# Turning the state-space input weights on TensorE: three rounded products of high and low parts in place of one in full precision

## The reference

```python
# 64 groups of 16 channels drive one 64-dim complex-diagonal state each
abar = exp(lam * dt);  f = (abar - 1) / lam
bb = f * B                        # (64 groups, 64 states, 16 channels), complex
s  = scan over time of  s[l] = abar * s[l-1] + bb @ u[l]
y  = Re(C @ s) + D * u            # then GELU and a sigmoid GLU
```

## Time and profile before

| what | value |
|---|---|
| median of three runs | 956.39 us |
| the profiled execution, its own time | 956.51 us |
| span of the profiled execution | 954.7 us |
| PE busy (matmul) | 933.3 us, 98% |
| DVE busy | 633.6 us, 66% |
| ACT busy | 349.0 us, 37% |
| mean granted TensorE clock | 0.999 |
| float32 matmuls of `part_a`, as records | 128 (96 into psa, 32 into psb) |

### The profile page before, as it was taken

How to read it: one execution, slowest core, us unless ns; L and a number is a source line. 1 busy time by engine, 2 the same in 40 slices (tenths; PEclk the granted TensorE clock), 3 DMA queues, 4 the chain that set the end, 5 groups by cost and what they waited for, 6 DMA issues and landing times.

```text
span 954.7 us, 11591 instructions
## 1 busy us (share of the span) xinstructions
PE 933.3 (98%) x4420; PEld 784.8 (82%) x4420; DVE 633.6 (66%) x904; ACT 349.0 (37%) x448; POOL 45.3 (5%) x82
## 2 busy tenths in 40 slices
PE   3999999999999999999999999999999999999997
PEld 3888888888888888888888888888888888888885
DVE  5988899877888884577677887665344444455233
ACT  5851353334444443345353535341022231223111
POOL 0019800000000000000000000000000000000000
PEclk9999999999999999999999999999999999999999
DMA  9843355446555354479474761696543258322222
GB/s 348 300 147 121 126 203 168 155 159 195 173 192 202 141 184 157 114 217 260 132 216 137 208 171 44 192 346 239 185 163 111 89 224 214 135 89 89 89 89 88
DMA packets 95143, 162.51 MB, mean 170 GB/s; under 512 B 38512, under 2 KB 55024, under 8 KB 95088
## 3 DMA queue, kind: packets, MB, share of 16 engines
q1 hardware_dynamic: 85728, 157.31, 50.4%
q10 hardware_dynamic: 9360, 4.46, 1.8%
HBM read 115.59 MB, written 46.14 MB: 169 GB/s over the span
## 4 chain that ended last, share of the span: by engine, by line
PE 97%; DVE 1%; DMA 1%; ACT 0%; SPq 0%; issue 0%; DVEq 0%
PE ps L1932 51%; PE ps L2052 18%; PE ps L2160 9%; PE psb L2052 8%; PE ps L2116 2%; PE psb L2105 1%; PE psb L2103 1%; PE psa L2091 1%; PE psa L2010 1%; PE psa L1932 1%; PE psb L1960 1%; DMA x_tok<-in_x 1%; PE ps L1960 0%; PE psb L2010 0%; PE psa L1960 0%; DVE par_w_p L534 0%
## 5 line engine op out<-in xcount | busy, mean ns | idle before, releaser
L1932 PE MATMUL ps<-bop,w_hi 128*128 128x512 f32 x1184 | 317.7, 390 | 0.2 <-DVE bop L1440 0.2
L1932 PEld LDWEIGHTS ps<-bop,w_hi 128*128 128x128 f32 x1184 | 221.3, 188 | 45.6 <-issue 0.3
L1932 PE MATMUL ps<-bop,w_lo 128*128 128x512 f32 x592 | 182.3, 389 | 0.0
L1932 PEld LDWEIGHTS ps<-bop,w_lo 128*128 128x128 f32 x592 | 111.1, 188 | 23.2
L1392 DVE TENSOR_TENSOR w_lo<-raw,w_hi 128x1024 fp32r<-128x1024 f32 x45 | 55.6, 1236 | 48.5 <-ACT w_hi L1010 48.4
L2052 PE MATMUL ps<-bop,r_hi 128*128 128x512 f32 x256 | 78.8, 389 | 0.0
L1010 ACT ACTIVATE w_hi<-raw 128x1024 fp32r<-128x1024 f32 x45 | 47.4, 1054 | 75.7 <-PE ps L1932 61.9
L2052 PEld LDWEIGHTS ps<-bop,r_hi 128*128 128x128 f32 x256 | 48.0, 188 | 10.0
L2052 PE MATMUL ps<-bop,r_lo 128*128 128x512 f32 x128 | 49.8, 389 | 0.0
L2160 PE MATMUL ps<-wo_hi,y_hi 128*128 128x512 f32 x128 | 49.8, 389 | 0.0
L2160 PE MATMUL ps<-wo_lo,y_hi 128*128 128x512 f32 x128 | 49.8, 389 | 0.0
(11 more groups left out here) (325 smaller groups left out, 1582.3 us busy)
## 6 DMA issues: line engine op xcount, KB each, us to landing
raw<-in_wstream SPq DMA_DIRECT2D x54, 512.0 KB, 4.5
pair_raw<-in_wstream SPq DMA_DIRECT2D x24, 512.0 KB, 4.2
ada<-in_w_ada SPq DMA_DIRECT2D x16, 512.0 KB, 11.5
x_tok<-in_x SPq DMA_DIRECT2D x8, 512.0 KB, 6.3
gs_d<-gt SPq DMA_DIRECT2D x8, 512.0 KB, 4.3
win_d<-win_new SPq DMA_DIRECT2D x8, 512.0 KB, 2.7
wout_d<-wout_new SPq DMA_DIRECT2D x8, 512.0 KB, 3.8
wout<-wout_d SPq DMA_DIRECT2D x8, 512.0 KB, 6.0
```

Source lines behind the costliest of these rows:

```text
L1932: last = mm(ps[slot(u)][:, f * HALF:f * HALF + HALF], a[:, k, :], b(k, f), start=k == order[0] and q == 0, stop=k == order[-1] and q == 2)
```

## The change

`v` and the C columns get a high and a low part. ACT rounds `v` to `v_hi` at the end of the iteration in which DVE made it; DVE subtracts to get `v_lo`, in the place of `v`, in the next iteration between `pair_low` P3 and the chunk at "a"; DVE makes `c_lo`, 128 x 128, right behind `v`. The identity and the high part of C are now of type fp32r. PE does three matmuls for each group: `v_hi` with [identity, C_hi] (144 columns), `v_lo` with the same (144 columns), `v_hi` with `C_lo` (16 columns, into the tap columns alone). `v_hi` lies where `vt` was, so `out_weights` takes a new scratch `wt`, at the place of `win_new`; for that reason it waits for the store of `win_new` before it, and `prep_out` on ACT now waits for `wout_ready`. The calls of `prep_out` and `part_a` at place "a", where no "in" chunk ever falls, are gone.

```diff
+        v_hi = at("v_hi", [P, GB, CH, SG], bop_at + 5 * TILE, F32R)
+        v_lo = at("v_lo", [P, GB, CH, SG], bop_at + 4 * TILE, F32R)
         win_new = at("win_new", [P, GB, P], p1[0])
+        wt = at("wt", [P, GB, CH, SG], p1[0])
...
+        c_lo = ssm("c_lo", [P, GB, SG], F32R)
...
-        eye_c = at("eye_c", [P, GB, P + SG], cur[0])
+        eye_c = at("eye_c", [P, GB, P + SG], cur[0], F32R)
...
+            def v_high(chunk):
+
+                if chunk is None or chunk[0] != "in":
+                    return
+                act.wait_ge(v_ready, chunk[1] + 1)
+                fn(v_hi[:, :, :, :], v[:, :, :, :], ACT.Copy).then_inc(v_hi_done, 1)
...
                 act.wait_ge(a_done, b + 1)
+                act.wait_ge(wout_ready, b + 1)
...
-                prep_out(CHUNK_AT.get((j, "a")))
...
                 if more:
                     pair_high(j + 1, P6)
+                v_high(CHUNK_AT.get((j, "b")))
...
-                    dve.wait_ge(wout_ready, KT)
+                    dve.wait_ge(a_done, KT)
...
                 tt(v[:, :, :, :], v[:, :, :, :], vt4, ALU.add).then_inc(v_ready, 1)
+                stt(c_lo[:, :, :], bc[:, 2, :, :], sign, eye_c[:, :, P:P + SG].bitcast(F32), ALU.mult, ALU.subtract).then_inc(v_lo_done, 1)
+
+            def in_weights_low(chunk):
+
+                if chunk is None or chunk[0] != "in":
+                    return
+                dve.wait_ge(v_hi_done, chunk[1] + 1)
+                tt(v_lo[:, :, :, :], v[:, :, :, :], v_hi[:, :, :, :].bitcast(F32), ALU.subtract).then_inc(v_lo_done, 1)
...
                 dve.wait_ge(wout_stored, 16 * b)
+                dve.wait_ge(cos_stored, 16)
+                dve.wait_ge(win_stored, 16 * b)
...
-                did(tt(vt4, bcast(cf[:, :, 24:32], 3, SG), bcast(bc[:, 3, :, :], 2, CH), ALU.mult))
+                did(tt(wt[:, :, :, :], bcast(cf[:, :, 24:32], 3, SG), bcast(bc[:, 3, :, :], 2, CH), ALU.mult))
                 do(tt(w, bcast(cf[:, :, 16:24], 3, SG), bcast(bc[:, 2, :, :], 2, CH), ALU.mult))
-                tt(w, w, vt4, ALU.add).then_inc(wout_ready, 1)
+                tt(w, w, wt[:, :, :, :], ALU.add).then_inc(wout_ready, 1)
...
                     pair_low(j, P3)
+                in_weights_low(CHUNK_AT.get((j - 1, "b")))
                 prepare(CHUNK_AT.get((j, "a")))
...
-                pe.wait_ge(v_ready, b + 1)
+                pe.wait_ge(v_lo_done, 2 * b + 2)
...
-                    vg = v[:, g, :, :].rearrange("p j h -> p (j h)")
+                    vh, vl = (z[:, g, :, :].rearrange("p j h -> p (j h)") for z in (v_hi, v_lo))
                     bank, at_ = turned[g]
-                    last = mm(bank[:, at_:at_ + P + SG], vg, eye_c[:, g, :], start=True, stop=True)
+                    mm(bank[:, at_:at_ + P + SG], vh, eye_c[:, g, :], start=True, stop=False)
+                    mm(bank[:, at_:at_ + P + SG], vl, eye_c[:, g, :], start=False, stop=False)
+                    last = mm(bank[:, at_ + P:at_ + P + SG], vh, c_lo[:, g, :], start=False, stop=True)
...
-                part_a(CHUNK_AT.get((j, "a")))
```

More of the change, by code:

```diff
@@ L404, in build @@
         pair_stored = two("pair_stored")
+        v_hi_done, v_lo_done = sem("v_hi_done"), sem("v_lo_done")
         v_ready, eye_ready, a_done, win_ready, win_stored = (sem("v_ready"), sem("eye_ready"), sem("a_done"),
```

## The result

The changed kernel took 962.52 us (median of four runs, 962.21 to 962.83) against 956.50 us for the kernel before, measured beside it: a ratio of 1.0063, 95% interval 1.0045 to 1.0080. It is slower by 6.0 us. The profiled execution took 962.52 us with a span of 960.5 us.

A forecast was written before the change was run, and what follows sets the result against it. PE's instruction pace was taken as the bound: 64 groups going from 245.0 to 333.9 ns add 5.7 us, ACT, DVE and queues nothing, giving 962.1 us. The range was 953.0 to 966.0, the likeliest case's own 961.3 to 965.7.

The forecast's parts named there:

- PE is the bound, and a change counts by PE's pace: Whole kernel: PE is 97% of the chain; a change counts by PE pace or by making PE wait.
- Each product at 111.3 ns: Bursts on PE: three products at the load-bound float32 pace, 333.9 ns a group against 245.0, +5.7 us over 64.
- The bound of 130 ns from one turn of type: Turn from float32 to fp32r on PE: load and handing over take 130 ns at most, 390 ns a group, +9.3 us.
- The rival of the hidden load: Three products of a burst: load takes 73 ns or less, kernel gains 5.0 to 1.6 us; chance 0.17.
- the even one: Products of a burst: a pace of 77 to 87 ns each keeps the difference within 1.1 us; chance 0.07.
- The rival without a single pass: Short fp32r products on PE: four passes like float32, +29.9 us (986) or +22.8 us (979); chance 0.05.
- The 0.06 us behind each burst as a price of changing type, taken as 0: Two half products behind each burst: 5.50 us against 5.44; if a type-change price, 0.5 us would go; taken as 0.
- ACT and DVE at nothing: v_hi 1.05 us on ACT, v_lo 1.24 and c_lo 0.28 on DVE: costed at nothing, working ahead of PE.
- the queue of SP at nothing: Stores of win_new and wout_new, loads of cf and bc: move by 0.7 to 1.2 us, costed at nothing.
- the faster rival: Three products of a burst: the load hides behind a short fp32r stream, 951.4 to 954.8 us; chance 0.17.
- The rival of the late `v_lo`: Top of each burst: PE waits for v_lo; 0.5 us at each of eight adds 4 us, 966; chance 0.06.

The follow-up runs named there:

- third_144: Changed kernel with the third product of each group moving 144 columns (identity and C_hi) in place of 16; 962.2 us, ratio 1.0061 to the kernel before.
- third_32cols: Changed kernel with the third product's stationary side 32 columns of v_hi in place of 128; 958.7 us, ratio 1.0028 to the kernel before.
- no_third: Changed kernel with the third product of each group (v_hi with C_lo, 16 columns) left out; 956.03 us, ratio 0.9997 to the kernel before.
- side_only: Changed kernel with its ACT and DVE work and waits, but one float32 product per group on PE; 956.82 us against 956.31 for the kernel before.
- v_lo_thrice: Changed kernel with two more operations of v_lo's size on DVE ahead of v_lo; 988.03 us, ratio 1.0324 to the kernel before.

## Why the prediction was right, step by step

The prediction said 962.1, the measured time is 962.52; against its own executions +5.7 was forecast and +6.0 measured, +5.8 by the spans.

- **PE is the bound, and a change counts by PE's pace.** Held: the 5.67 us of the loop are eight times the 0.71 of a burst.
- **Each product at 111.3 ns, the 16-column one too, 333.9 ns a group.** Held: 335 ns. That the load sets it was argued from two facts, that a load shrank as much as a two-pass stream between the slow and the fast stretch, and that an fp32r load is as long as a float32 one. third_144, third_32cols and no_third show it.
- **The bound of 130 ns from one turn of type.** Safe but loose: the pace measured is 111.8, and the 122.5 ns stream of the float32 record ahead would account for most of the 130.
- **The rival of the hidden load, and the even one.** Both fall. The stream alone would allow some 68 ns for 144 columns, which third_32cols laid bare, and the load's 112 stands above it. The fast weight load of the Trainium skill ("TensorE: Matmul & The Clock Gate", weight-path perf modes) did not show itself for fp32r: its load of 128 columns takes two cycles a column by the rows at half clock, and its record is as long as that of float32. The some 81 ns that the same page of the Trainium skill gives for a load and matmul pair of 128 columns (back-to-back issue gap) is not the pace here either: 111.8 ns.
- **The rival without a single pass.** Falls: 64 records more, not 256.
- **The 0.06 us behind each burst as a price of changing type, taken as 0.** Taking it as 0 was right. third_144 has no float32 product in the loop and its half products behind the burst still take 5.50 us, and in the changed kernel burst and half products exceed 24 x 111.8 + 5440 ns by 0.05. What slows them is open.
- **ACT and DVE at nothing.** Right for this kernel, and the weakest step; in part it was luck. `v_lo` ended 1.3 us ahead of the first weight load in most bursts, 1.1 in the seventh and 0.46 in the sixth, where I had 1.2 and 0.5. `prep_out` waited for `wout_new` once, behind the sixth burst. Its eviction began 3.38 us after the burst's first matmul in place of 2.78, 0.6 us later, where I had 0.5 at most:

```profile
279.39 1.23 DVE L1587 TENSOR_TENSOR wout_new<-wout_new,wt 128x1024 f32<-128x1024 f32 x1
...
280.70 0.81 ACT L1195 ACTIVATE win_new<-psa 128x768 f32<-128x768 f32 x1 [3.96 <-PE psb L2037]
```

The view puts this wait down to PE, whose burst had ended at 280.06. I looked at each of these delays by itself and not at the loop that they close, from `v_lo` over `wout_new` and the eviction to the next `v_lo`. In side_only that loop takes 21.37 us; that the iteration became 21.77 us long, and not less, is what kept it harmless. And I costed the queue of SP at nothing because "the end of the iteration moves by 0.7 too"; that was true only of the burst that I forecast. side_only shows 0.9 us of lateness without the longer burst. My range for a lesser burst, the faster rival, should have carried that price.
- **The rival of the late `v_lo`.** It did not happen, so its chance needs no defence, but its price was wrong: I took PE's wait as the whole cost. v_lo_thrice shows that waits of 9.9 us brought 8.5 more through the clock in the best execution, so by that run a wait is to be priced at about twice its length, and 966 should have been more. Waits as short as the 0.5 us of this rival were not tried.

## What to carry to other kernels

Price a short matmul by the longer of its stream and its weight load: here 112 ns for 128 stationary columns in fp32r (float32 records of 128 columns come 111 ns apart too). So a rounded product of 16 to 160 moving columns gains nothing from fewer columns (up to some 240 by an estimate, 111.8 ns less 11, at 2.4 GHz), and three of them lose to one float32 product of 144 columns (two loads, both hidden). Put columns that share a stationary side under one load. When work is added to engines off the chain, look for the loop from one iteration to the next through evictions, queues, landings and the waits that the change itself adds, and compare its length with the iteration that the change itself will give, not with today's.

## What the runs showed of the hardware that I had not expected

- A wait of PE costs more than its length: after waits of 0.9 to 2.1 us in an otherwise saturated stretch the granted clock went to 0.50 for 3 to 7 us in three of eight cases, while five waits of 0.7 to 1.5 us had no such effect. What decides is open.
- PE's wait row understates a lateness: in side_only the weight loads waited 1.8 us for `v_lo` and the loop grew by 0.9, while the matmul row named no such wait.
- The stream of an fp32r product has an overhead at full clock (13.4 ns at 512 columns, 11 at 288, some 8 at 144). It isn't constant; whether it grows with the columns or by something else was not tried.
- The half products behind a burst of short products run at 232 ns a matmul in place of 227 for the first dozen. It was there before the change and after it.
